# A two-layer hybrid encoder on one Trainium2 core: the first lap of three weight streams takes both slabs in step, and the r mixing moves into its norm

## The reference

```python
mod = jax.nn.silu(c) @ mod_w[i] + mod_b[i]
sh_m, sc_m, g_m, sh_f, sc_f, g_f = [m[:, None, :] for m in jnp.split(mod, 6, axis=-1)]
h = rms_norm(x, norm_g[i, 0]) * (1 + sc_m) + sh_m
...
xx = token_shift(h) - h
mixed = h[None] + xx[None] * mu[:, None, None, :]
xr, xw, xk, xv, xa, xg = mixed[0], mixed[1], mixed[2], mixed[3], mixed[4], mixed[5]
r = xr @ w_r
w_log = -jax.nn.softplus(-(w0 + jnp.tanh(xw @ w1) @ w2)) - 0.5
...
h = rms_norm(x, norm_g[i, 2]) * (1 + sc_f) + sh_f
u = h @ w_in
```

## Time and profile before

| what | us |
|---|---|
| median of 3 runs (lowest and highest) | 3054.93 (3046.2 to 3060.29) |
| the profiled execution, device time | 3052.57 |
| its span in the trace | 3050.8 |
| PE busy in that span | 2815.7 (92%) |
| DVE busy | 2049.9 (67%) |
| ACT busy | 1414.0 (46%) |
| POOL busy | 143.6 (5%) |

### The profile page before, as it was taken

How to read it: one execution, slowest core, us unless ns; L and a number is a source line. 1 busy time by engine, 2 the same in 40 slices (tenths; PEclk the granted TensorE clock), 3 DMA queues, 4 the chain that set the end, 5 groups by cost and what they waited for, 6 DMA issues and landing times.

```text
span 3050.8 us, 61351 instructions
## 1 busy us (share of the span) xinstructions
PE 2815.7 (92%) x23950; PEld 2563.5 (84%) x23950; DVE 2049.9 (67%) x2682; ACT 1414.0 (46%) x1971; POOL 143.6 (5%) x160
## 2 busy tenths in 40 slices
PE   2399999899999999997999999998989999999998
PEld 2299999878888889996988778886978888889998
DVE  6878887797786666557865554553786666665555
ACT  0134443455555554446754333332446666664343
POOL 0000000100000000000000223130100000000000
PEclk8599999999999999998999999998999999999999
DMA  8788887867776658782655332332856666656775
GB/s 293 260 282 306 277 292 274 292 208 248 243 233 185 186 175 259 228 255 89 194 186 180 121 125 78 111 99 77 306 191 192 186 185 186 186 182 219 234 247 168
DMA packets 502583, 628.22 MB, mean 206 GB/s; under 512 B 26904, under 2 KB 435336, under 8 KB 502152
## 3 DMA queue, kind: packets, MB, share of 16 engines
q1 hardware_dynamic: 498368, 622.62, 62.7%
q10 hardware_dynamic: 4040, 3.07, 0.3%
HBM read 623.50 MB, written 2.10 MB: 205 GB/s over the span
## 4 chain that ended last, share of the span: by engine, by line
PE 86%; DVE 8%; DMA 2%; ACT 2%; issue 2%; ACTq 0%; SPq 0%; DVEq 0%
PE ps L1886 28%; PE ps L1902 27%; PE ps L1905 14%; PE ps L2096 11%; DVE macc L1252 3%; PE ps L1920 1%; PE ps L1929 1%; DMA raw<-in_fox_w_in 1%; DVE wlo L1230 1%; PE ps L2150 1%; PE ps L1992 1%; DMA crow<-in_ffn_conv_b 0%; PE ps L1995 0%; DVE mx L1582 0%; PE ps L2077 0%
## 5 line engine op out<-in xcount | busy, mean ns | idle before, releaser
L1230 DVE TENSOR_TENSOR wlo<-raw,whi 128x1024 fp32r<-128x1024 f32 x792 | 970.3, 1231 | 572.1 <-ACT whi L798 571.1
L798 ACT ACTIVATE whi<-raw 128x1024 fp32r<-128x1024 f32 x792 | 832.2, 1058 | 915.4 <-PE ps L1905 312.7
L1902 PE MATMUL ps<-xs,whi 128*128 128x512 f32 x3328 | 1178.6, 399 | 28.8 <-DVE xs L1589 15.0
L1905 PE MATMUL ps<-xs,wlo 128*128 128x256 f32 x3328 | 934.5, 281 | 0.0
L1902 PEld LDWEIGHTS ps<-xs,whi 128*128 128x128 f32 x3328 | 628.1, 189 | 185.2 <-issue 27.0
L1886 PE MATMUL ps<-act,whi 128*128 128x256 f32 x3840 | 705.3, 287 | 24.3 <-DVE wlo L1230 24.2
L1886 PEld LDWEIGHTS ps<-act,whi 128*128 128x128 f32 x3840 | 609.6, 195 | 26.3 <-DVE wlo L1230 26.3
L1905 PEld LDWEIGHTS ps<-xs,wlo 128*128 128x128 f32 x3328 | 630.8, 190 | 0.0
L1886 PE MATMUL ps<-act,wlo 128*128 128x256 f32 x1920 | 549.0, 286 | 0.0
L1886 PEld LDWEIGHTS ps<-act,wlo 128*128 128x128 f32 x1920 | 374.8, 195 | 0.0
L1252 DVE SCALAR_TENSOR_TENSOR macc<-raw,cact,macc 128x1024 f32<-128x1024 f32 (+1 forms) x280 | 331.2, 1183 | 6.3 <-DMA raw<-in_mod_w 1.4
(11 more groups left out here) (266 smaller groups left out, 2973.8 us busy)
## 6 DMA issues: line engine op xcount, KB each, us to landing
raw<-in_ffn_w_in SPq DMA_DIRECT2D x352, 512.0 KB, 4.0
raw<-in_mod_w SPq DMA_DIRECT2D x256, 512.0 KB, 5.2
raw<-in_ffn_w_out SPq DMA_DIRECT2D x176, 512.0 KB, 4.7
raw<-in_fox_w_in SPq DMA_DIRECT2D x96, 512.0 KB, 5.8
raw<-in_mod_w SPq DMA_DIRECT2D x128, 384.0 KB, 4.9
raw<-in_fox_w_out SPq DMA_DIRECT2D x32, 512.0 KB, 7.1
raw<-in_mod_w SPq DMA_DIRECT2D x64, 256.0 KB, 4.5
raw<-in_rwkv_w_r SPq DMA_DIRECT2D x32, 512.0 KB, 4.4
```

The lines of the kernel that those rows point to most:

```text
L798: sc.activation(whi[:, half, :, :].rearrange("p k n -> p (k n)"), slots[slot], ACT.Copy).then_inc(w_hi, 1)
L1230: v.tensor_tensor(wlo[:, half, :, :].rearrange("p k n -> p (k n)"), slots[slot], whi[:, half, :, :].rearrange("p k n -> p (k n)").bitcast( ...
L1902: pe.matmul(ps[bank + m][:, :], whi[:, half, k, m * P:m * P + P], src[:, kt, :, :].rearrange("p u s -> p (u s)"), start=kt == 0, stop=Fals ...
L1905: last = pe.matmul(ps[bank + m][:, 0:S], wlo[:, half, k, m * P:m * P + P], src[:, kt, 0, :], start=False, stop=kt == KT - 1, skip_group_ch ...
```

## The change

Three first laps are rearranged: of the up projection in both feed-forward parts, and of the r projection.

- PE (`first_slabs`) takes the pieces of the two slabs in turn: input tiles 0 to 3 of slab 0, then 0 to 3 of slab 1, then 4 to 7 of slab 0, and so on. SP loads the pieces in that order. Each slab is then complete only after piece 6 and piece 7 (counted from 0), and `side` waits for piece 6.
- Pieces 4 to 7 are split (ACT `hi`, DVE `lo`) between the groups of the norm, where they stood behind the whole norm (`ahead = 8`).
- In norm 2, ACT and DVE make mixture 0 of a group as soon as the group stands; the scaled tiles get a buffer of their own (`tbm`, 8 tiles).
- In the layer 0 up projection, whose three laps are one pattern, the 16 M steps stand behind pieces 8 to 21 of the 24, where they stood behind pieces 4 to 21.

```diff
-    ph_up[0] = Phase(UP_GROUPS, "WWWW" + spread(UP_GROUP * 8 - 6, KT, "M") + "WW", early=4)
+    ph_up[0] = Phase(UP_GROUPS, "W" * 8 + spread(UP_GROUP * 8 - 10, KT, "M") + "WW", early=4)
...
+    ph_up[0].ahead = ph_up[1].ahead = ph_r.ahead = 8
...
+        tbm, _ = at("tbm", O_V, [P, 8, S])
...
                     def one(i):
-                        stream(ph, i, lambda w: w_up[n][:, 4 * (w % 4):4 * (w % 4) + 4,
-                                                        ds(i * (per * SLAB) + ((lap0 + w // 8) * SLAB + (w // 4 % 2) * FF),
-                                                           SLAB)], 1, 0)
+                        def src(w):
+                            q, half = (w // 2, w % 2) if lap0 == 0 and at_start(i, w - 7) else (w % 4, w // 4 % 2)
+                            return w_up[n][:, 4 * q:4 * q + 4,
+                                           ds(i * (per * SLAB) + ((lap0 + w // 8) * SLAB + half * FF), SLAB)]
+
+                        stream(ph, i, src, 1, 0)
...
-                    piece(ph_r, 0, R_AT[i] + w, w_rkv[0][:, 4 * (w % 4):4 * (w % 4) + 4,
-                                                         (2 * i + w // 4) * SLAB:(2 * i + w // 4 + 1) * SLAB])
+                    q, half = (w % 4, w // 4) if i else (w // 2, w % 2)
+                    piece(ph_r, 0, R_AT[i] + w, w_rkv[0][:, 4 * q:4 * q + 4,
+                                                         (2 * i + half) * SLAB:(2 * i + half + 1) * SLAB])
...
-                if not (at_start(i, 0) and w < ph.early):
+                if not (at_start(i, 0) and w < max(ph.early, ph.ahead)):
...
+            def x_hi(n, ph=None):
...
                     last.then_inc(*s["a"].inc(f"hi{r_}"))
+                    if ph and 3 <= r_ < 7:
+                        hi(ph, 0, r_ + 1)
...
-                def side(i, half):
-
-                    sc.wait_ge(w_used, up_weight(n, i, 4 * half + 3))
+                def side(i, half, first=False):
+
+                    sc.wait_ge(w_used, up_weight(n, i, 6 + half if first else 4 * half + 3))
                     sc.activation(ub[:, 2 * half:2 * half + 2, 2:S + 2], duo[half][:, :, S:2 * S],
...
-            def mix_first():
+            def norm_and_mix():
+
                 for g in range(9):
                     if g < 8:
+                        sc.wait_ge(*norm[2]["v"].at(f"t{g}"))
+                        for t in (2 * g, 2 * g + 1):
+                            last = sc.activation(hb[:, t, 1:S + 1], tbm[:, t % 8, :], ACT.Identity, bias=shift_col(2, t))
+                        last.then_inc(*norm[2]["a"].inc(f"hi{g}"))
                         if g >= 4:
                             sc.wait_ge(*mix_lo.at("lo", g - 4))
+                        sc.wait_ge(*norm[2]["a"].at(f"hi{g}"))
                         mixed_now(0, g, g % 4)
                     if g:
                         mixed_hi(0, g - 1, (g - 1) % 4)
+                    if 4 <= g < 8:
+                        hi(ph_r, 0, g)
 
             def side(j, i, s, used):
...
-                        side(0, i, 0, ph_r.weight(0, R_AT[i] + 3))
+                        side(0, i, 0, ph_r.weight(0, R_AT[i] + (3 if i else 6)))
...
+            def x_norm(n, ph=None):
...
+                    if n == 2:
+                        if 1 <= r_ < 9:
+                            mixed_sum(0, r_ - 1, (r_ - 1) % 4)
+                        if r_ >= 2:
+                            mixed_lo(0, r_ - 2, (r_ - 2) % 4)
+                    if ph and 4 <= r_ < 8 and n != 2:
+                        lo(ph, 0, r_)
+                    if ph and 5 <= r_ < 9 and n == 2:
+                        lo(ph, 0, r_ - 1)
 
                 if n == 2:
-                    v.wait_ge(*s["a"].at("hi7"))
-                    v.wait_ge(*s["v"].at("t7"))
...
+            v.memset(hb[:, :, 0:1], 0.0).then_inc(*mix_zero.inc("zero"))
+            v.wait_ge(*mix_zero.at("zero"))
+            x_norm(2, ph_r)
...
+            def first_slabs(ph, src, ready):
+
+                for w in range(8):
+                    half = ph.half(w)
+                    pe.wait_ge(raw_done, ph.done(0, ph.w_at[w]))
+                    for k in range(PIECE_KT):
+                        kt = PIECE_KT * (w // 2) + k
+                        if w % 2 == 0 and k % 2 == 0:
+                            pe.wait_ge(*ready(kt // 2))
+                        for m in range(2):
+                            bank = ps[2 * (w % 2) + m]
+                            pe.matmul(bank[:, :], whi[:, half, k, m * P:m * P + P],
+                                      src[:, kt, :, :].rearrange("p u s -> p (u s)"), start=kt == 0, stop=False,
+                                      skip_group_check=True)
+                            last = pe.matmul(bank[:, 0:S], wlo[:, half, k, m * P:m * P + P], src[:, kt, 0, :],
                                              start=False, stop=kt == KT - 1, skip_group_check=True)
                     last.then_inc(w_used, 1)
...
-                    paired_slab(ph, j, w0, 0, xs, ready=(lambda r_: norm[2 * n + 1]["v"].at(f"lo{r_}")) if first else None)
+                    if first:
+                        first_slabs(ph, xs, lambda r_: norm[2 * n + 1]["v"].at(f"lo{r_}"))
+                        return
+                    paired_slab(ph, j, w0, 0, xs)
                     paired_slab(ph, j, w0 + 4, 2, xs)
...
-                paired_slab(ph_r, 0, R_AT[i], 0, xs, ready=None if i else lambda r_: mix_lo.at("lo", r_))
-                paired_slab(ph_r, 0, R_AT[i] + 4, 2, xs)
+                if i:
+                    paired_slab(ph_r, 0, R_AT[i], 0, xs)
+                    paired_slab(ph_r, 0, R_AT[i] + 4, 2, xs)
+                else:
+                    first_slabs(ph_r, xs, lambda r_: mix_lo.at("lo", r_))
```

More of the change, by code:

```diff
@@ L1011, in body @@
                                 sc.wait_ge(*s["z"].at("zero"))
-                            side(i, 0)
+                            side(i, 0, first)
                 up_laps(sc, n, body)
@@ L1065, in lora_out @@
                 sc.activation(dst, src, func).then_inc(*lo_a.inc(name))
-            sc.wait_ge(*norm[2]["a"].at("hi7"))
-            mix_first()
+            norm_and_mix()
             for i in range(4):
@@ L1267, in pieces @@
                         if 0 <= w < last:
-                            if not (at_start(i, 0) and w0 + w < ph.early):
+                            if not (at_start(i, 0) and w0 + w < max(ph.early, ph.ahead)):
                                 lo(ph, i, w0 + w)
@@ L1567, in _ @@
             x_root(1)
-            x_norm(1)
+            x_norm(1, ph_up[0])
             up_proj(0)
@@ L1856, in _ @@
             x_root(3)
-            x_norm(3)
+            x_norm(3, ph_up[1])
             up_proj(1)
@@ L1905, in paired_slab @@
                             last = pe.matmul(ps[bank + m][:, 0:S], wlo[:, half, k, m * P:m * P + P], src[:, kt, 0, :],
+                                             start=False, stop=kt == KT - 1, skip_group_check=True)
+                    last.then_inc(w_used, 1)
+            def first_slabs(ph, src, ready):
[12 more added lines that the diff above has]
+                            last = pe.matmul(bank[:, 0:S], wlo[:, half, k, m * P:m * P + P], src[:, kt, 0, :],
                                              start=False, stop=kt == KT - 1, skip_group_check=True)
```

24 lines of the change are left out of this document (7 added, 17 removed).

## The result

The changed kernel takes 3064.38 us (median of 12 runs, 3052.15 to 3075.97), the kernel before 3047.30 beside it (12 runs, 3043.80 to 3060.29). The medians lie 17.1 us apart and the means 13.3; the ratio of the runs is 1.0041, 95% interval 1.0025 to 1.0057, which is about 12.5 us slower, 7.6 to 17.4. The profiled execution took 3055.27 us, span 3053.5.

The account below looks back on a forecast made before the run. PE was taken as the bound, except from norm 2 to the first LoRA, where DVE sets the end. Up laps +1.1 and +2.4 and r +4.7 made +8.2 us, forecast 3062 us, range 3047 to 3075.

Parts of the forecast that it names:

- Waits in the up laps: Up projections: ACT loses its lead, PE waits before pieces 8 and 10; +1.1 us layer 0, +2.4 layer 1.
- the second wait: Up projections, before piece 10: PE waits again for ACT and DVE; 0.8 us in layer 1, 0.83 in layer 0.
- the third rival: Layer 0 up laps: denser M steps stop PE some 3 us in each of four groups; +12, 3075; chance 0.11.
- The r part: Norm 2 and r: PE starts 6.2 us earlier, the LoRA 2.5 later, plus 2.2 for clock; +4.7 us.
- the handovers: Mixture 1 before the LoRA: single groups go between DVE and ACT in turn, 2.4 us each against 1.4 work.
- The low clock: LoRA: PE comes out of the wait before it at half clock; 2.2 us, taken from 1.4 to 2.6.
- The first rival: At r the head start stays, -7.1 us, with up laps +3.5: -3.6, 3051; chance 0.17.
- the norm is already fast enough for PE: Both up laps: the norm keeps up with PE, so only the wait before the first group could be won.
- the low clock behind the 5.4 us waits: Up laps: PE runs at 0.50 after the gap before the first matmul; costs 1.4 to 2.6 us.

Follow-up runs that it names:

- up_only: Changed kernel with norm 2 and r put back as before, so only the up projections are changed; ratio 1.0016, 3057.66 us.
- up_hoist: Changed kernel with ACT's high part of piece 8 issued ahead of the first `side`, layer 1's lap 1 written out; ratio 1.0044, 3066.90 us.
- r_pipe: Changed kernel with mixture 1's groups scaled ahead, one group's scaling beside the next one's mixing; ratio 1.0035, 3064.65 us.
- warm: Changed kernel with 20 extra matmuls that nobody reads on PE inside the wait before the first LoRA; ratio 1.0045, 3065.93 us.
- r_back: Changed kernel with the splits of pieces 4 to 7 back among the groups of mixture 1; ratio 1.0028, 3061.42 us.
- fill_before: Kernel before with products nobody reads added in PE's waits ahead of norm sums, up and down projections, k and v; ratio 1.0008, 3052.15 us.
- r_only: Changed kernel with both up projections put back as before, keeping the new r and norm 2; ratio 1.0020, 3060.07 us.

## Why the prediction was right, and where it wasn't

I forecast 3062 us, +8.2, in a range of 3047 to 3075; measured were 3064 and +12.5 (7.6 to 17.4). That the two absolute times lie so close is in part luck: mine stood on a median of three runs, 3054.93, where twelve give 3047.30; on these, +8.2 would have been 3055.5.

**Waits in the up laps: right.** 1.5 and 0.8 us forecast for layer 1, 1.61 and 0.48 found; 0.25 and 0.83 for layer 0, 0.18 and 0.47 found. So the second wait was put too long in both, by 0.3 to 0.4 us. `up_only` has them without the new r, `up_hoist` loses the first of each pair. With the pace out the projections are 2.6 and 1.9 us longer (2.4 and 1.1 forecast); of the 1.9 in layer 0 some 0.6 is the clock behind the first wait, which happened to be 0.50 in both changed executions. No further wait came in layer 0, so the third rival, M steps that are too dense, is out. In this place the switch of the table cost ACT 1.28 us and nothing beside it: `side` ends and the load begins at 2296.9, and `hi` begins 0.02 us behind it. The Trainium skill (ScalarE: Activation LUTs, What ACT_TABLE_LOAD costs) has a drain of some 1.38 us on top; the changed trace doesn't show it either. By that figure the wait would, as an estimate, have been 3 us.

**The r part: right in the mechanism and the sum.** PE started r after 8.86 us of waiting where it had waited 14.99, so it won 6.1 us (6.2 forecast), stood 9.92 us before the LoRA (9.6) and began it 2.4 us later than before (2.5). `r_pipe` shows that the handovers are the reason, since the lag goes to 0.1 us without them. Moving the splits back among mixture 1, where they filled DVE's idle time, gives half of the lag back; pipelining the handovers gives all of it. The low clock cost 1.8 us, or 2.1 with the slow pace in it (2.2 forecast), shown by `warm` and by `r_back`, where the wait is elsewhere and the LoRA stretch takes 27.9. The first rival, that the head start stays, is out: in the kernel before DVE was busy for all of the 25.53 us from the first r matmul to the LoRA, and nothing of its work was removed.

**What the first reading had wrong.** "In both up laps, then, the norm is already fast enough for PE": it is fast enough only for a PE at reduced clock. With the wait filled, PE ran into DVE's 1.58 us a group. So the low clock behind the 5.4 us waits costs 0.1 us where it is granted 0.71 and about 1.5 where it is 0.50 (42 matmuls in the first 10 us of the first profile, 52 and 53 in the others), not 1.4 to 2.6. In the sum the term stood twice: in the start times of pieces, where it did no harm, and as the range from which I took 2.2 us for the LoRA, where no norm feeds PE piece by piece and it held. It made my expectation for `fill_before` too large.

**What the sum left out.** The prediction puts nothing between the LoRA stretch and the second up projection. By the stretches with the pace out, k and v together came out 1.9 us longer and the recurrence 2.8, and that is, to 0.2 us, the difference between the parts that were forecast (1.9 + 2.6 + 1.8 + 2.6 = 8.9) and the 13.4 from the table. For k and v the difference is the clock behind their waits: with 0.66 over its first 5 us k took 93.48, with 1.00 91.91, and with 0.50 94.7 (`warm`), each at the quick pace. But it comes and goes: it is low in 3 of 10 windows with the old r, in 11 of 14 with the new one, in none of four with the wait filled. Whether the change makes it more frequent stays open.

The recurrence took 411 to 414 us in six executions with the old r and 413 to 417 in eight with the new. Its length goes with the granted clock as well. Over the whole of it (columns as above, the clock third from the end), in the kernel before, `fill_before`, the changed kernel and `r_only`:

```profile
1728.11:2140.05 411.94, 373.94 (x7680) 318.81 (x7680) 204.31 (x419) 128.73 (x292) 96.08 (x128) 0.95 0.31 97
1729.33:2140.52 411.19, 371.36 (x7681) 316.20 (x7681) 203.47 (x419) 128.47 (x292) 95.69 (x126) 0.96 0.30 97
1733.19:2150.30 417.11, 380.28 (x7681) 325.27 (x7681) 203.67 (x419) 128.75 (x292) 95.91 (x128) 0.93 0.29 96
1734.93:2152.27 417.34, 380.45 (x7680) 325.40 (x7680) 202.81 (x419) 128.61 (x292) 95.24 (x126) 0.93 0.29 96
```

The three longest of the 14 (416.0 to 417.3) are those with the clock at 0.93, and where it was 0.95 the two kinds of r were about 1 us apart in the mean (411.9 to 414.2 with the old, 413.8 to 414.6 with the new). So what the sum left out lies, as far as the traces tell, for the most part in time at the lower clock behind the LoRA. Nothing was run that holds the recurrence's clock fixed: that the clock makes the length is argued and not shown, and why it was lower in some executions stays open. The measured interval holds the 8.2 of the forecast too, so the runs by themselves don't call for these 4.7 us.

## What to carry to other kernels

An engine that starts earlier wins nothing if what it needs next is the end of another engine's queue: add up that engine's work to the point of the next dependency, handovers included, and the wait that comes up there can be forecast to half a microsecond. A wait that has only been moved can cost more than before, because PE may come out of it at a lower clock. And before a few microseconds are read from a total, look how far two executions of the same kernel lie apart, and compare stretches instead.
